# Two of eight residual additions behind two post norms, moved from VectorE to GpSimd

## The chip, the core and the metric

The kernel runs on one core of one Trainium2 chip. The metric is the device time of one execution in microseconds (us). The core has five instruction streams: TensorE (PE, matmuls; PEld, its weight loads), VectorE (DVE), ScalarE (ACT), GpSimd (POOL) and SyncE (SP, which issues the DMAs here). Each runs its own program in order, and they wait for each other on semaphores.

## The reference

Two blocks of a network are computed in a row on x of 512 tokens by 1024 features, in float32. What matters here are the residual sums of the first block, each behind a norm, and each followed by the norm and the projection of the next part:

```
x = x + rmsnorm(merged @ w_out, norm_mix_post)     # first sum
h = rmsnorm(x, norm_ffn_pre)
up = h @ w_up                                       # then a conv, a gelu gate and w_down give f
x = x + rmsnorm(f, norm_ffn_post)                   # second sum
proj = rms_norm(x, norm_a) @ w_in_a                 # start of the second block
```

rmsnorm(x) is x / sqrt(mean of x*x over the features + 1e-6), times a gain for each feature.

## The kernel before, in words

**Layout.** x lies turned in SBUF as X, [128 partitions, 8, 512]: eight "rows" m of 128 features each (the partitions), with the 512 tokens along the free dimension. "The fourth and the sixth row" are m = 3 and m = 5.

**Matmuls in three passes.** Each float32 product is made of three fp32r passes: high*high, low*high and high*low. For X that gives the pair HH (high half, made by ScalarE in `a_high`, L2086) and HL (low half, made by VectorE in `v_low`, L1273, from X and HH). Each weight block of 128 by 128 is split too: 512 KB units of eight blocks are loaded into `raw` by SyncE, ScalarE casts WH, and VectorE subtracts to get WL. TensorE needs all four.

**The norm.** The gain goes into HH and HL, and the factor 1/sqrt(...) of a token is put on after the projection, by multiplying with RS. So TensorE can start on the projection before the squares are summed. ScalarE writes the square of each row (`a_square`, L2090) into a ring SQ of two tiles (row 0 straight into SQS), GpSimd adds them up in SQS (`g_sum`, L2718), and TensorE sums SQS over the partitions (`pe_norm`).

**The stage that the change touches** is `v_post` (L1301) on VectorE with `a_post` (L2133 on) on ScalarE and `g_sum` on GpSimd. It runs twice: for "mix post" (first sum, F = FA, then the projection "ffn") and for "ffn post" (second sum, F = FB, then the projection "a"). First the factor row of the post norm is made and laid out over the partitions in PSUM (`ps("nr", st)`). Then, for each row m, VectorE computes

- TT(m) = F(m) * gain(m) * factor row, into a ring TT of two tiles (L1324),
- X(m) = X(m) + TT(m) (L1327), which it waits for its own TT(m) for,
- HL(m-1) (L1329), which needs HH(m-1) of ScalarE,

and in between, where the weight plan (`prepare`, called by `ahead` and `tile`) says so, one WL. ScalarE does HH(m) and the square of X(m), while m < 5 also a copy PW of a finished side product out of PSUM, and WH where the plan says so. GpSimd adds the square of row m to SQS. Every engine's order is fixed by the program.

**TensorE meanwhile** does eight small side tiles (`pe_post`), and then starts the next projection with a loop that takes the rows k = 0 to 7 of H one after the other, for four output tiles at once (`first` for "ffn", `tokens4` for "a"): 4 tiles x 3 passes = 12 matmuls for each k, each k waiting for HL(k) ("lo ffn" or "lo a"). The rest of the projection follows tile by tile.

**Semaphores.** Every engine has one counter (S.dve, S.act, S.pool, S.pe); `then_inc` raises it and records under the names given at which count a result is there; `wait_ge(S.dve, "x ffn", m)` waits for that count. `free(...)` names when a buffer has been read; `take` and `fill` wait for it. Each DVE, ACT and POOL instruction is made in a shared helper, so the profile's lines are those of the helpers: L151 tensor_tensor, L163 scalar_tensor_tensor, L188 copies and casts, L201 activations, L204 matmuls, L208 transposes.

Of the kernel before, what the change touches and what calls it, by code (L numbers as in the profile page):

```python
# [11 lines left out]
MUL, ADD, SUB, MAX, MIN = ALU.mult, ALU.add, ALU.subtract, ALU.max, ALU.min  # L12

P = 128
T = 512
# [542 lines left out]
def free(*name):  # L558
    return ("free", name if len(name) > 1 or isinstance(name[0], str) else name[0])


def build(nc, a_in):
    with ExitStack() as ctx:
        S = Signals(nc, ctx)
# [4 lines left out]
        def at(name, shape, dt, off=None):  # L569
            size = 4  # L570
            for d in shape[1:]:
                size *= d
            if off is None:
                off = pos[0]
                pos[0] += (size + 31) // 32 * 32
                assert pos[0] <= top, (name, pos[0], top)
            assert off + size <= top, (name, off + size, top)
            t = nc.alloc_sbuf_tensor_at(name, list(shape), dt, offset=off)
            return t[tuple(slice(None) for _ in shape)]
# [8 lines left out]
        X = at("X", [P, 8, T], F32)  # L588
        HH = at("HH", [P, 8, T], F32R)
# [77 lines left out]
        def c(name, i=0, p0=0, p1=P):  # L667
            k = COL[name] + i
            return cv[p0:p1, k:k + 1]
# [4 lines left out]
        def ring(kind, buf):  # L674
            return lambda *name: buf[:, S.place.get((kind, name), 0), :]

        tt_, sq_, th_, rt_, ct_ = ring("T", TT), ring("Q", SQ), ring("TH", TH), ring("RT", RT), ring("CT", CT)

        def col_(*name):
            k = 64 + 4 * S.place.get(("COL", name), 0)  # L680
            return sm[:, k:k + 4]
# [78 lines left out]
        def pe_columns(p, name, qs, consumed):  # L760

            s = p.fill(name[0], name[1])
            for t in range(4):
                for n, (q, sig, key) in enumerate(qs):
                    p.wait_ge(sig, *key)
                    p.matmul(s[:, t:t + 1], q[:, t * P:(t + 1) * P], ones[:, 0:1], n == 0, n == len(qs) - 1)
            p.then_inc(name[1], *consumed)

        def pe_squares(p, bank, name, sig, key, sq, consumed):

            s = p.fill(bank, name)
            p.wait_ge(S.ident, "ident")
            p.wait_ge(sig, *key)
            for t in range(4):
                p.transpose(s[:, t * P:(t + 1) * P], sq[:, t * P:(t + 1) * P], ident)
            p.then_inc(name, *consumed)

        def v_squares(v, name, col):
            v.wait_ge(S.pe, *name)
            v.tensor_reduce(col, ps(*name).rearrange("p (t s) -> p t s", s=P), ADD).then_inc(("sum",) + name, free(name))  # L780

        def pe_row(p, bank, name, col, key, consumed=()):

            s = p.fill(bank, name)
            p.wait_ge(S.ident, "ident")
            p.wait_ge(S.dve, *key)
            for t in range(4):
                p.transpose(s[:, t * P:(t + 1) * P], col[:, t:t + 1].to_broadcast([P, P]), ident)
            p.then_inc(name, *consumed)

        NORM_USE = {"a": "downed 1"}

        def pe_norm(p, st):
            def columns():
                if st in NORM_USE:
                    yield pe_squares(p, SB[4], ("nc", st), S.pool, ("sqs", st, 7), SQS, [free("sqs", st)])
                yield pe_columns(p, (SB[4], ("nc", st)), [(SQS, S.dve if st == "mix" else S.pool, ("sqs", st, 7))], [free("sqs", st)])

            p.wait_ge(S.dve, "ones")
            if st in ("p0", "p1"):  # L800
                p.mid.append(columns())
            else:
                next(columns())
            for _ in range(5 if st == "ffn" else 1):
                yield
            pe_row(p, SB[4], ("nr", st), RC, ("rc", st))
# [471 lines left out]
        def v_column(v, name, col):  # L1278
            v.wait_ge(S.act, name[0] + " sqrt", *name[1:])
            v.reciprocal(col, col).then_inc(name)  # L1280
# [20 lines left out]
        def v_post(v, st, F, post, nxt, gain):  # L1301
            v.tile(2)
            v.take("COL", ("post", st))
            v.take("COL", ("post 7", st))
            col, col7 = col_("post", st), col_("post 7", st)
            v_squares(v, ("nc", st), col)
            v_squares(v, ("nc7", st), col7)
            v.wait_ge(S.dve, "sum", "nc", st)
            v.wait_ge(S.dve, "sum", "nc7", st)
            v.tensor_tensor(col, col, col7, ADD).then_inc(("post sum", st), free("COL", ("post 7", st)))  # L1310
            v_column(v, ("post col", st), col)
            for m in range(1, 3):
                v.tile(2)
            for m in range(8):
                v.ahead(m, 4)
                v.take("T", (st, m))
                v.wait_ge(S.pe, "nr", st)
                if st == "mix post":
                    v.wait_ge(S.act, "f", m)
                    v.wait_ge(S.y[m // 2], "y")  # L1320
                else:
                    v.wait_ge(S.dve, "f2", m)
                    v.wait_ge(S.dve, "x ffn", m)
                v.scalar_tensor_tensor(tt_(st, m), F[:, m, :], c(post, m), ps("nr", st), MUL,  # L1324
                                       MUL).then_inc(("post", st, m), *([free("nr", st)] * (m == 7)))
                v.wait_ge(S.dve, "post", st, m)
                v.tensor_tensor(X[:, m, :], X[:, m, :], tt_(st, m), ADD).then_inc(("x " + nxt, m), free("T", (st, m)))  # L1327
                if m:
                    v_low(v, nxt, m - 1, gain, HH, HL)  # L1329
                if 3 <= m < EARLY:  # L1330
                    v.tile(2)
            v_low(v, nxt, 7, gain, HH, HL)
            v.soon.append(v_norm(v, nxt))
# [72 lines left out]
        def dve_program(v):  # L1406
# [292 lines left out]
            def residual(st, nk, n, x_key, nxt, gain, layer, between=None):  # L1699
                v.first(nk, n, between)  # L1700
                for m in range(8):
                    if m < n:
                        v.taken()
                    else:
                        v.tile(nk)
                    v.wait_ge(S.pe, "res", st, m)
                    v.wait_ge(S.dve, "x " + x_key, m)
                    v.tensor_tensor(X[:, m, :], X[:, m, :], ps("res", st, m), ADD).then_inc(("x " + nxt, m), free("res", st, m))
                    if m:
                        v_low(v, nxt, m - 1, gain, HH, HL)  # L1710
                v_low(v, nxt, 7, gain, HH, HL)
# [374 lines left out]
        def a_high(a, st, k, gain, hi, x_sig, *x_key):  # L2086
            a.wait_ge(x_sig, *x_key)
            a.activation(hi[:, k, :], X[:, k, :], ACT.Copy, scale=c(gain, k)).then_inc(("hi " + st, k))
# [46 lines left out]
        def a_post(a, st, nxt, gain, fin, use, layer):  # L2135
            a.tile(2)
            a.wait_ge(S.dve, "post sum", st)
            a.activation(col_("post", st), col_("post", st), ACT.Sqrt, scale=1.0 / D, bias=c("eps")).then_inc(("post col sqrt", st))
            for m in range(3):
                if m:  # L2140
                    a.tile(2)
                a_keep(a, layer, m)
            for m in range(8):
                a.ahead(m, 4)
                if m == 0:
                    a.wait_ge(S.pe, "mark", fin[0], *fin[1:])
                a_high(a, nxt, m, gain, HH, S.dve, "x " + nxt, m)
                a_square(a, nxt, m, X[:, m, :], ("sqs", st))
                if m + 3 < EARLY:
                    a.tile(2)  # L2150
                    a_keep(a, layer, m + 3)
            a.soon.append(a_norm(a, nxt, use))
# [562 lines left out]

        def g_sum(g, st, n=8):  # L2718

            for k in range(1, n):  # L2720
                g.wait_ge(S.act, "sqs in", st, k)
                if k > 1:
                    g.wait_ge(S.pool, "sqs", st, k - 1)
                g.tensor_tensor(SQS, SQS, sq_(st, k), ADD).then_inc(("sqs", st, k), free("Q", (st, k)))
# [10 lines left out]
        def pool_program(g):  # L2735
# [104 lines left out]
            g.mark("mixed")  # L2840
            g.mark("fa")
            g_sum(g, "mix post", 7)
            g_sum(g, "ffn")
            g.mark("fb")
            g_sum(g, "ffn post", 7)
            g_sum(g, "a")
            g.mark("a")
            g.wait_mark("a")
            for half in range(2):
# [377 lines left out]
```

## Time and profile before

| what | value |
| --- | --- |
| median of 3 runs | 1392.41 us (1392.0 to 1392.72) |
| the profiled execution | 1393.89 us, its span 1392.0 us |
| PE busy | 1381.5 us, 99% of the span |
| PEld busy | 1125.8 us, 81% |
| DVE busy | 841.2 us, 60% |
| ACT busy | 604.6 us, 43% |
| POOL busy | 180.3 us, 13%, 149 instructions |
| granted TensorE clock | nine tenths or more of full speed in each of 40 slices |

The profile is of one execution. The span is the time between its first and its last recorded instruction; the execution's own time is 1.89 us more. Durations of single instructions come from this execution. The releaser behind an arrow is what ended an engine's idle time. Matmuls overlap (one is recorded at 0.39 us, and the next starts 0.23 us after it), so starts say more than durations on TensorE.

### The profile page before, as it was taken

The numbers are of one execution on the slowest core, as the hardware profiler recorded it, in microseconds if no ns is written. First come the engines' busy times: TensorE is split into PE (matmuls) and PEld (weight loads), VectorE is DVE, ScalarE is ACT, GpSimd is POOL, SyncE is SP. The second block draws the span as 40 slices with busy tenths as digits, with TensorE's granted clock in tenths as the row PEclk, the third lists the DMA queues.
The fourth block names the chain that finished last, engine by engine and source line by source line (L and its number), as shares of the span: only waits on it lengthen the run. The fifth ranks groups of instructions, "written<-read, shape, count | busy, mean of one in ns | idle before, by whom it ended". The sixth has DMA issues, their size and how long they took to land.

```text
span 1392.0 us, 17342 instructions
## 1 busy us (share of the span) xinstructions
PE 1381.5 (99%) x6816; PEld 1125.8 (81%) x6816; DVE 841.2 (60%) x1223; ACT 604.6 (43%) x924; POOL 180.3 (13%) x149
## 2 busy tenths in 40 slices
PE   8999999999999999999999999999999999999998
PEld 7777777878888788888888887888888888787887
DVE  5656555755342798624676456646455565877774
ACT  5264433423235554423444345434544544344561
POOL 0300010212212300000000112000001120233330
PEclk9999999999999999999999999999999999999999
DMA  6321322222352433332333324322125233222141
GB/s 207 106 91 50 97 68 76 71 82 76 104 169 91 136 91 108 99 113 83 99 93 105 106 78 151 112 86 76 61 61 169 88 119 106 82 61 61 47 145 68
DMA packets 37554, 135.39 MB, mean 97 GB/s; under 512 B 4432, under 2 KB 5344, under 8 KB 36960
## 3 DMA queue, kind: packets, MB, share of 16 engines
q1 hardware_dynamic: 37472, 134.28, 30.5%
q8 instruction: 54, 0.88, 0.3%
q14 instruction: 28, 0.23, 0.1%
HBM read 127.97 MB, written 6.29 MB: 96 GB/s over the span
## 4 chain that ended last, share of the span: by engine, by line
PE 93%; DVE 4%; DMA 2%; issue 1%; ACT 0%; SPq 0%; DVEq 0%; ACTq 0%
PE ps L204 90%; PE ps L208 3%; DVE WL L151 1%; DVE TT L163 1%; DMA X<-in_xT 1%; DVE HL L163 1%; DMA raw<-in_wall 1%; DVE X L151 1%; SPq L211 0%; ACT WH L188 0%; DVE QT L163 0%; DVE PU L151 0%; DVE TT L157 0%; DVE sm L169 0%; DVE TT L151 0%
## 5 line engine op out<-in xcount | busy, mean ns | idle before, releaser
L204 PE MATMUL ps<-HH,WH 128*128 128x512 f32 (+1 forms) x1096 | 440.3, 402 | 2.7 <-DVE HL L163 2.0
L204 PE MATMUL ps<-HH,WL 128*128 128x512 f32 (+1 forms) x1096 | 426.1, 389 | 0.0
L204 PE MATMUL ps<-HL,WH 128*128 128x512 f32 (+1 forms) x1096 | 425.4, 388 | 0.0
L151 DVE TENSOR_TENSOR WL<-raw,WH 128x1024 fp32r<-128x1024 f32 (+1 forms) x223 | 285.8, 1286 | 85.0 <-ACT WH L188 83.9
L188 ACT CAST WH<-raw 128x1024 fp32r<-128x1024 f32 (+1 forms) x223 | 231.5, 1040 | 135.1 <-PE ps L204 112.6
L204 PEld LDWEIGHTS ps<-HH,WH 128*128 128x128 f32 x1096 | 206.1, 188 | 52.8 <-issue 8.2
L204 PEld LDWEIGHTS ps<-HH,WL 128*128 128x128 f32 x1096 | 205.8, 188 | 43.8 <-DVE WL L151 0.3
L204 PEld LDWEIGHTS ps<-HL,WH 128*128 128x128 f32 x1096 | 206.3, 188 | 41.3 <-issue 1.7
L204 PE MATMUL ps<-PH,WH 128*128 128x512 f32 x424 | 167.6, 395 | 0.0
L204 PE MATMUL ps<-PH,WL 128*128 128x512 f32 x424 | 165.2, 390 | 0.0
L204 PE MATMUL ps<-PL,WH 128*128 128x512 f32 x424 | 165.1, 389 | 0.0
L151 POOL TENSOR_TENSOR SQS<-SQS,SQ 128x512 f32<-128x512 f32 x47 | 71.8, 1528 | 681.9 <-ACT SQ L201 681.3
L151 DVE TENSOR_TENSOR TH<-ps,RS 128x512 f32<-128x512 f32 (+1 forms) x93 | 63.6, 684 | 134.8 <-PE ps L204 126.9
L204 PEld LDWEIGHTS ps<-PH,WH 128*128 128x128 f32 x424 | 79.6, 188 | 17.1 <-issue 1.0
L204 PEld LDWEIGHTS ps<-PH,WL 128*128 128x128 f32 x424 | 79.6, 188 | 16.8
L204 PE MATMUL ps<-WH,HH 128*128 128x512 f32 x224 | 92.2, 411 | 0.6 <-DVE HL L163 0.6
L204 PEld LDWEIGHTS ps<-PL,WH 128*128 128x128 f32 x424 | 79.7, 188 | 15.8
L204 PE MATMUL ps<-WL,HH 128*128 128x512 f32 x224 | 87.5, 391 | 0.0
L204 PE MATMUL ps<-WH,HL 128*128 128x512 f32 x224 | 87.3, 390 | 0.0
L201 ACT ACTIVATE TH<-TH 128x512 f32<-128x512 f32 (+1 forms) x41 | 25.5, 621 | 107.5 <-DVE TH L151 107.4
L163 DVE SCALAR_TENSOR_TENSOR CT<-TH,cv,CT 128x511 f32<-128x511 f32 x88 | 65.8, 747 | 6.4 <-ACT CT L201 4.9
L201 ACT ACTIVATE CT<-TH,cv 128x512 f32<-128x512 f32 x44 | 36.0, 817 | 56.7 <-DVE TH L151 54.9
(222 smaller groups left out, 1456.2 us busy)
## 6 DMA issues: line engine op xcount, KB each, us to landing
raw<-in_wall SPq DMA_DIRECT2D x221, 512.0 KB, 3.6
kept<-PW SPq DMA_DIRECT2D x2, 2048.0 KB, 9.1
PWR<-kept SPq DMA_DIRECT2D x2, 2048.0 KB, 8.4
X<-in_xT SPq DMA_DIRECT2D x8, 256.0 KB, 4.0
X<-in_xT SPq DMA_DIRECT2D x4, 512.0 KB, 4.7
out_T<-X SPq DMA_DIRECT2D x7, 256.0 KB, 2.0
pe<-in_pT SPq DMA_DIRECT2D x2, 512.0 KB, 4.9
DM<-in_dm SPq DMA_DIRECT2D x1, 640.0 KB, 4.2
```

Source lines behind the costliest of these rows:

```text
L151: return self.put(None if self.e is None else self.e.tensor_tensor(out, x, y, op))
L163: return self.put(self.e.scalar_tensor_tensor(out=out, in0=x, scalar=s, in1=y, op0=op0, op1=op1))
L188: return self.put(None if self.e is None else self.e.copy(out, x))
L201: return self.put(self.e.activation(out, x, f, **kw))
L204: return self.put(None if self.e is None else self.e.matmul(out, l, r, start=start, stop=stop, skip_group_check=True))
L208: return self.put(None if self.e is None else self.e.transpose(out, x, ident[0:k, 0:k]))
```

## The change

VectorE no longer adds rows 3 and 5 of X in the two stages. GpSimd does, in its own queue just ahead of the step that adds the square of that row to SQS, once VectorE's TT of the row is there. Who reads these two rows then waits for GpSimd's counter in place of VectorE's: ScalarE's HH(3) and HH(5) (L2147), the second `v_post`, which reads the X of the first (L1323), and the later residual sum of part "a" (L1707). All other rows, and the order of everything else, are as before.

```diff
+        POOL_ROWS = (3, 5)
...
@@ v_post
                     v.wait_ge(S.dve, "f2", m)
-                    v.wait_ge(S.dve, "x ffn", m)
+                    v.wait_ge(S.pool if m in POOL_ROWS else S.dve, "x ffn", m)
                 v.scalar_tensor_tensor(tt_(st, m), F[:, m, :], c(post, m), ps("nr", st), MUL,
                                        MUL).then_inc(("post", st, m), *([free("nr", st)] * (m == 7)))
-                v.wait_ge(S.dve, "post", st, m)
-                v.tensor_tensor(X[:, m, :], X[:, m, :], tt_(st, m), ADD).then_inc(("x " + nxt, m), free("T", (st, m)))
+                if m not in POOL_ROWS:
+                    v.wait_ge(S.dve, "post", st, m)
+                    v.tensor_tensor(X[:, m, :], X[:, m, :], tt_(st, m), ADD).then_inc(("x " + nxt, m), free("T", (st, m)))
@@ residual (VectorE)
-                    v.wait_ge(S.dve, "x " + x_key, m)
+                    v.wait_ge(S.pool if x_key == "a" and m in POOL_ROWS else S.dve, "x " + x_key, m)
@@ a_post
-                a_high(a, nxt, m, gain, HH, S.dve, "x " + nxt, m)
+                a_high(a, nxt, m, gain, HH, S.pool if m in POOL_ROWS else S.dve, "x " + nxt, m)
@@ g_sum
-        def g_sum(g, st, n=8):
+        def g_sum(g, st, n=8, post=None):
             for k in range(1, n):
+                if post and k in POOL_ROWS:
+                    g.wait_ge(S.dve, "post", post, k)
+                    g.tensor_tensor(X[:, k, :], X[:, k, :], tt_(post, k), ADD).then_inc(("x " + st, k), free("T", (post, k)))
                 g.wait_ge(S.act, "sqs in", st, k)
@@ pool_program
-            g_sum(g, "ffn")
+            g_sum(g, "ffn", post="mix post")
...
-            g_sum(g, "a")
+            g_sum(g, "a", post="ffn post")
```

## Rows read from the trace of the kernel before

**Rows 1.** The chain of work that ended last, its share of the span by engine.

```profile
PE 93%; DVE 4%; DMA 2%; issue 1%; ACT 0%; SPq 0%; DVEq 0%; ACTq 0%
```

**Rows 2.** Busy time: stretch, length, PE, PEld, DVE, ACT, POOL, PEclk, DMA, GB/s.

```profile
451.90:478.00 26.10, 25.52 (x111) 20.50 (x110) 25.65 (x29) 16.99 (x27) 11.81 (x7) 1.00 0.27 81
```

**Rows 3.** Timeline of TensorE, first stage: start, length in us, what, idle before.

```profile
471.88 0.39 PE L204 MATMUL ps<-HH,WL 128*128 128x512 f32 x1
472.27 0.50 PE L204 MATMUL ps<-HH,WH 128*128 128x512 f32 x1
...
474.91 0.39 PE L204 MATMUL ps<-HH,WL 128*128 128x512 f32 x1
475.87 0.47 PE L204 MATMUL ps<-HH,WH 128*128 128x512 f32 x1 [0.57 <-DVE HL L163]
```

**Rows 4.** Timeline of VectorE, first stage: WL, TT(3), X(3), HL(2), WL, X(4), and on.

```profile
457.44 2.32 DVE L151 TENSOR_TENSOR WL<-raw,WH 128x1024 fp32r<-128x1024 f32 x1
459.69 0.73 DVE L163 SCALAR_TENSOR_TENSOR TT<-FA,cv,ps 128x512 f32<-128x512 f32 x1
460.45 1.01 DVE L151 TENSOR_TENSOR X<-X,TT 128x512 f32<-128x512 f32 x1
461.39 0.74 DVE L163 SCALAR_TENSOR_TENSOR HL<-X,cv,HH 128x512 fp32r<-128x512 f32 x1
462.05 1.21 DVE L151 TENSOR_TENSOR WL<-raw,WH 128x1024 fp32r<-128x1024 f32 x1
...
463.96 1.01 DVE L151 TENSOR_TENSOR X<-X,TT 128x512 f32<-128x512 f32 x1
...
466.32 0.69 DVE L151 TENSOR_TENSOR X<-X,TT 128x512 f32<-128x512 f32 x1
466.93 1.78 DVE L163 SCALAR_TENSOR_TENSOR HL<-X,cv,HH 128x512 fp32r<-128x512 f32 x1
...
470.54 1.02 DVE L151 TENSOR_TENSOR X<-X,TT 128x512 f32<-128x512 f32 x1
471.48 0.74 DVE L163 SCALAR_TENSOR_TENSOR HL<-X,cv,HH 128x512 fp32r<-128x512 f32 x1
...
474.99 1.62 DVE L163 SCALAR_TENSOR_TENSOR HL<-X,cv,HH 128x512 fp32r<-128x512 f32 x2
```

**Rows 5.** Timeline of ScalarE, first stage: HH(4), SQ(4), PW, WH, HH(5).

```profile
465.00 0.72 ACT L201 ACTIVATE HH<-X,cv 128x512 fp32r<-128x512 f32 x1 [1.78 <-DVE X L151]
465.63 0.62 ACT L201 ACTIVATE SQ<-X 128x512 f32<-128x512 f32 x1
466.15 0.57 ACT L188 COPY PW<-ps 128x512 f32<-128x512 f32 x1
466.62 1.05 ACT L188 CAST WH<-raw 128x1024 fp32r<-128x1024 f32 x1
467.57 0.72 ACT L201 ACTIVATE HH<-X,cv 128x512 fp32r<-128x512 f32 x1
```

**Rows 6.** Timeline of GpSimd, first stage: SQS(2), SQS(3), SQS(4).

```profile
458.95 1.97 POOL L151 TENSOR_TENSOR SQS<-SQS,SQ 128x512 f32<-128x512 f32 x1 [0.27 <-ACT SQ L201]
462.82 1.60 POOL L151 TENSOR_TENSOR SQS<-SQS,SQ 128x512 f32<-128x512 f32 x1 [1.91 <-ACT SQ L201]
466.33 1.84 POOL L151 TENSOR_TENSOR SQS<-SQS,SQ 128x512 f32<-128x512 f32 x1 [1.91 <-ACT SQ L201]
```

**Rows 7.** GpSimd's other adds into X (min/median/max ns), and two timelines near 264 us.

```profile
L151 POOL TENSOR_TENSOR X<-X,TT x16: 1290/2200/2208, 264.2 to 406.2; 128x512 f32<-128x512 f32 x16
...
264.71 1.99 DVE L151 TENSOR_TENSOR gqks<-GQK,gE 128x1024 f32<-128x1024 f32 x1 [0.23 <-PE ps L204]
...
264.22 1.40 POOL L151 TENSOR_TENSOR X<-X,TT 128x512 f32<-128x512 f32 x1 [40.38 <-DVE TT L163]
265.59 2.17 POOL L151 TENSOR_TENSOR gE<-gb 128x256 f32<-128x256 f32 x2
```

**Rows 8.** Timeline of TensorE, second stage: the first matmul of row group k=6.

```profile
849.71 0.47 PE L204 MATMUL ps<-WH,HH 128*128 128x512 f32 x1 [0.58 <-DVE HL L163]
```

## The prediction, made before the changed kernel was run

> **What bounds the kernel now.** I read the chain that ended last first [rows 1]: TensorE holds 93% of it. Its matmuls follow each other every 0.227 us at the full clock of 2.4 GHz (granted 1.00 in the stage of [rows 2]), so the end of the kernel moves only where TensorE waits. The change touches two such places, the stretches behind the two sums: 451.90 to 478.00 us and 825.70 to 852.00 us. In [rows 2], the first of them, VectorE is busy for 25.65 of 26.10 us there and GpSimd for 11.81: VectorE is what the first tiles of the next projection wait for. [Rows 3] show it at TensorE, whose first loop takes the rows k of H in turn, twelve matmuls for each (four tiles of three passes). The last of k=4 starts at 471.88, so k=5 could start at 472.11; it starts at 472.27, 0.05 after HL(5) ends at 472.22 [rows 4]. Its twelve matmuls end their starts at 474.91, so k=6 could start at 475.14; it starts at 475.87, released by HL of row 6. That is 0.16 + 0.73 = 0.89 us lost. The second stage is a copy 373.84 us later: its TensorE wait is the same, at 849.71 [rows 8]. So **the most that the change can gain is 2 x 0.89 = 1.8 us**, 0.13% of the time, and what it can lose has no such limit. About 0.2% (2.8 us) is what a measurement can tell from no change.
>
> **Who waits for whom inside the stage.** For each row m VectorE does TT(m) (post norm), X(m), and HL(m-1), with WL (the low half of a weight unit) in between; ScalarE does HH(m) and the square SQ(m) after X(m); GpSimd adds SQ(m) into SQS. [Rows 4] give the lengths: TT 0.73, X 0.69, HL 0.74, WL 1.21. The next instruction starts 0.08 before the end of the last, but X starts 0.77 after TT starts, since it needs TT's result.
> The same rows hold a second fact. X(3) takes 1.01, HL(4) 1.78, one WL 2.32. Beside them stand GpSimd's adds [rows 6]: SQS(2) runs to 460.92, and X(3) ends 0.54 later, at 461.46; SQS(4) runs to 468.17, and HL(4) ends at 468.71. The other way, SQS(3), asked for at 462.82, ends 1.16 after the WL that ends at 463.26, and SQS(4) 1.16 after X(5), which ends at 467.01. TT, which reads PSUM and one tile of SBUF, stays at 0.73 beside a running add. So **an instruction of VectorE with two SBUF inputs and an add of GpSimd exclude each other**: one that waits on VectorE ends 0.55 after GpSimd's end (1.09 with 1024 columns, as WL: gqks at 264.71 ends 1.08 after the add that ends at 265.62, [rows 7]), one that waits on GpSimd 1.16 after VectorE's end. When both stand in line, the one that asked first gets it: HL(4), asked 466.93, lost to SQS(4), asked 466.33 [rows 4, 6]; and at 264.71 VectorE's gqks got in ahead of GpSimd's next add, asked 265.59 [rows 7].
>
> **The parts of the change.** *Removed:* X(3) and X(5) from VectorE, 2 x 0.69 in each stage. Without them HL(m-1) can follow TT(m) at 0.66 in place of 0.77 + 0.61, so 2 x 0.72 = 1.4 us of VectorE's queue goes. *Added:* the same two additions on GpSimd. Its add of the same tiles takes 1.29 undisturbed and 2.20 in the median [rows 7]; I take 1.29 and work the waiting out. *Moved:* X(3) stands between SQS(2) and SQS(3), X(5) between SQS(4) and SQS(5), so the squares' adds queue behind them, and HH(3) and HH(5), which ScalarE runs in order, now wait for GpSimd; with HH(5) everything behind it waits: SQ(5), a weight cast WH and HH(6). No DMA is moved. *Waits added:* VectorE waits on GpSimd's count before rows 3 and 5 of the second sum and of the later residual; those X are hundreds of us old, so between 0 and 0.03 us each (the gap from the end of X(4), 464.97, to the start of the HH(4) that it releases, 465.00 [rows 4, 5]), and I take 0. TT(5) and TT(7) now need GpSimd to have read TT(3) and TT(5): by the working below they are read at 462.6 and 471.3 and rewritten at 466.5 and 475.0, so nothing waits.
>
> **The replay of the first stage**, with these durations, from TT(3) on, which still starts at 459.69 [rows 4].
> HL(2) is asked for at 460.36, waits for SQS(2) (end 460.92), ends 461.47. GpSimd's X(3), next in its queue, was asked before WL (461.39) and ends at 461.47 + 1.16 = 462.63. WL ends 1.09 later, 463.72 (before: 463.26). HH(3) can start at 462.66, 1.2 us after the old X(3)'s end; with the steps of [rows 5] (HH to SQ 0.63, SQ to the next 0.52, then PW 0.47, WH 0.95) SQ(3) ends at 463.95 and SQS(3) runs from 464.03 to 465.32. TT(4) starts 463.64; X(4), asked at 464.41, ends at 465.87 (before: 464.97). So **one row in, the stage is 0.9 us late, not early**: 0.45 + 1.2 + 0.8 of waiting against 0.7 saved.
> HL(3) 465.79 to 466.53. TT(5) starts 466.46; no X(5); HL(4) is asked at 467.13, its HH(4) being done at 466.63, and ends at 467.87. SQS(4), asked at 467.24, ends at 469.03. WL, asked at 467.80, ends at 470.12. X(5), asked at 469.0, ends at 471.28. TT(6) starts 470.04, X(6) is asked at 470.81 and ends at 471.83 (before: 471.56). HH(5) runs from 471.32 to 472.04, so HL(5) ends at 472.83 (before: 472.22). SQS(5), asked at 472.65, ends at 473.99; WL, asked at 472.76, ends at 475.08; TT(7) starts 475.00; SQS(6), asked near 474.7, ends at 476.24; X(7), asked at 475.77, at 476.79. HL(6) starts at 476.71, **1.72 us later than the 474.99** of [rows 4]. TensorE follows: k=5 starts 0.6 late, k=6 1.7 late, and HL(7), due at 480.3, is ready at 478.4.
> The contest of HL(4) and SQS(4) is close (0.1 us). Had SQS(4) won, the same rules put HL(5)'s end at 474.1 and HL(6)'s start at 476.9, 1.9 late. Both outcomes give 1.7 to 1.9.
> Behind HL(6) nothing absorbs it. The last WL ends 1.7 later, as does the norm's last square sum, and the norm row goes through TensorE, which is late by as much. TensorE's waits of [rows 3] and [rows 8] are for HL; I find none for a freed bank or for weights in either stage. SyncE's weight loads and the store of PW behind them wait for WL, and WL is late by no more than TensorE. So the delay goes to the end in full.
> **Sum:** 2 x 1.72 = 3.4 us, between 3.4 and 3.8. It stands against the profiled execution (span 1392.0, 1393.89 with what lies around it, 1.5 above the median of the three runs, 1392.41). Put on the median: **1395.8 us**, +0.25%.
> Beside these rows a rule of the Trainium skill (page GPSIMD Engine Reference, section Engine selection) advises VectorE for elementwise work, since GpSimd is about 2 times slower with two inputs; the trace has 1.29 against 0.69, which agrees. Charged as length alone it would give 4 x 0.60 = 2.4 us, less than the replay, which also counts the mutual waiting.
>
> **Rivals.**
> *A. The contests fall more kindly: +1.6.* The place is 461.4, where WL and GpSimd's X(3) both stand behind HL(2). If GpSimd's request really comes after WL's (it then starts its add later than its record), WL ends at 462.6, X(3) at 463.8, X(4) at 464.3, and the rest by the same rules: HL(5) in time for TensorE, HL(6) starting at 475.8. TensorE's k=6 is then 0.8 late: 1394.0. For it: starts on GpSimd are rough. Against: GpSimd's next add starts within 0.1 us of the last one's end (264.22 + 1.40, 265.59, [rows 7]), 0.4 us ahead of WL.
> *B. Not slower: VectorE gains its two slots and loses nothing for them.* The price is at most the 1.8 us of the waits in [rows 3]: 1390.6. The mechanism is that GpSimd's longer queue overlaps TT and ScalarE's waits and never stands ahead of VectorE; the point that decides is the start of HL(6): before 474.99 it gains, from 474.26 on down it gains all. For it: VectorE is full (25.65 of 26.10 us) while GpSimd is idle for over half [rows 2]. Against: the seven SQS adds already stretch a WL to 2.32 and HL(4) to 1.78, and HH(5) would still have to wait for GpSimd.
> The Trainium skill (Perfetto Trace Analysis, Optimizing Scalar/DVE Operations) says that moving work to GpSimd may make sense when VectorE is saturated, but that between these two it might not help, because of a shared port. By its first half this rival wins, by its second the forecast; the stretched rows speak for the second.
> *C. More than the replay: +5 to +8.* The k=6 wait grows from 0.7 to about 2.4 us. If the granted clock fell after it, matmuls at 1.2 GHz would follow at twice 0.227 us, so that every ten of them cost 2.3 us. Or a third wait appears behind the norm. For it: no wait of this length stands in these stages before. Against: the clock stays at 1.00 through the two waits of today [rows 2, 3].
> *D. The change does nothing visible* would need both sums' HL chains to have slack; [rows 3] show that they have none.
>
> **How the numbers follow.** Forecast 0.56, A 0.24 (with its neighbours, +0.5 to +2.6), B 0.08, C 0.12. Slower by over 0.2% (above 1395.2): most of the forecast's case and C, 0.60. Within 0.2%: A, the low end of the forecast and B, whose whole gain is under 2.8 us, 0.37. Faster: 0.03. The range leaves out B's best and most of C: 1392.2 to 1397.6. The forecast's own range is 1395.2 to 1396.6.
>
> **What would show it.** In the changed profile: two POOL X<-X,TT in each stage, recorded at 1.7 to 2.3 us; VectorE X down from eight to six per stage, the WL behind TT(3) stretched to about 2.3, the one behind HL(4) as well; ScalarE idle some 2.7 us before HH(5), released by POOL; HL(6) starting 1.7 later against the stage's start; TensorE's wait before k=6 at 1.9 to 2.4 us in place of 0.57, and one of about 0.6 before k=5. If HL(6) starts by 475.0, the exclusion or its order is wrong; if it is 1.7 late and the end is not 3.4 later, something downstream absorbs it.

## The result, and the profile after

The changed kernel takes 1395.71 us (median of 9 runs, 1395.39 to 1397.11) against 1392.72 us (9 runs, 1392.0 to 1394.92) for the kernel before: a ratio of 1.002 with a 95% interval of 1.0012 to 1.0028, or 1.7 to 3.9 us slower. 1395.8 us was forecast. The profiled execution took 1395.99 us, with a span of 1394.2 us.

In the table "k=5" and "k=6" are the starts of the first matmul that reads row 5 or row 6. The stages are measured from the start of their own TT(0), since the first stage begins at another time in every execution (450.6 to 452.9 us over the profiles of this study, more on that at the end).

| | before | after |
| --- | --- | --- |
| TT(0) of the first stage starts | 451.94 | 450.95 |
| TensorE's k=5 behind TT(0) | 20.33 | 20.83 |
| HL(6) behind TT(0) | 23.05 | 24.63 |
| TensorE's k=6 behind TT(0), first / second stage | 23.93 / 23.95 | 25.52 / 25.53 |
| from the first stage's TT(0) to the second's | 373.82 | 375.41 |
| from the second stage's TT(0) to the end of the span | 566.24 | 567.84 |

Each stage costs 1.59 or 1.60 us more, and all of it arrives at the next stage and at the end: 3.2 us. The span grew by only 2.2 because this execution reached the first stage 0.99 us earlier.

The timeline of TensorE in the first stage (start, length, what, idle before and its releaser), which answers to [rows 3]:

```profile
470.91 0.39 PE L204 MATMUL ps<-HH,WL 128*128 128x512 f32 x1
471.78 0.50 PE L204 MATMUL ps<-HH,WH 128*128 128x512 f32 x1 [0.48 <-DVE HL L163]
...
476.47 0.47 PE L204 MATMUL ps<-HH,WH 128*128 128x512 f32 x1 [1.67 <-DVE HL L163]
```

Two waits stand where there was one that the profile marked: 0.48 before k=5 and 1.67 before k=6, in place of 0.57. The second stage has the same (this answers to [rows 8]):

```profile
851.89 0.47 PE L204 MATMUL ps<-WH,HH 128*128 128x512 f32 x1 [1.66 <-DVE HL L163]
```

The busy time in the same stretch of the span as [rows 2]:

```profile
451.90:478.00 26.10, 23.95 (x105) 19.15 (x104) 25.56 (x26) 16.75 (x26) 14.11 (x9) 1.00 0.25 81
```

VectorE has fewer instructions in the stretch (26 against 29) and is as busy as before (25.56 us against 25.65). The stage lies 0.99 us earlier in this execution; a stretch of the same length that starts with its own TT(0), at 450.95, gives 25.52 and 26 as well. What was taken from VectorE came back as waiting inside its instructions, as its timeline shows, from TT(3) on; it answers to [rows 4]:

```profile
458.69 0.73 DVE L163 SCALAR_TENSOR_TENSOR TT<-FA,cv,ps 128x512 f32<-128x512 f32 x1
459.35 1.12 DVE L163 SCALAR_TENSOR_TENSOR HL<-X,cv,HH 128x512 fp32r<-128x512 f32 x1
460.39 2.31 DVE L151 TENSOR_TENSOR WL<-raw,WH 128x1024 fp32r<-128x1024 f32 x1
462.62 0.73 DVE L163 SCALAR_TENSOR_TENSOR TT<-FA,cv,ps 128x512 f32<-128x512 f32 x1
463.39 1.42 DVE L151 TENSOR_TENSOR X<-X,TT 128x512 f32<-128x512 f32 x1
...
466.05 0.74 DVE L163 SCALAR_TENSOR_TENSOR HL<-X,cv,HH 128x512 fp32r<-128x512 f32 x1
466.72 2.32 DVE L151 TENSOR_TENSOR WL<-raw,WH 128x1024 fp32r<-128x1024 f32 x1
...
469.73 1.00 DVE L151 TENSOR_TENSOR X<-X,TT 128x512 f32<-128x512 f32 x1
470.98 0.75 DVE L163 SCALAR_TENSOR_TENSOR HL<-X,cv,HH 128x512 fp32r<-128x512 f32 x1 [0.24 <-ACT HH L201]
471.64 2.32 DVE L151 TENSOR_TENSOR WL<-raw,WH 128x1024 fp32r<-128x1024 f32 x1
...
475.58 1.62 DVE L163 SCALAR_TENSOR_TENSOR HL<-X,cv,HH 128x512 fp32r<-128x512 f32 x2
```

And GpSimd's, which answers to [rows 6]: SQS(2), X(3), SQS(3), SQS(4), X(5), SQS(5).

```profile
457.96 1.96 POOL L151 TENSOR_TENSOR SQS<-SQS,SQ 128x512 f32<-128x512 f32 x1 [0.28 <-ACT SQ L201]
459.88 1.74 POOL L151 TENSOR_TENSOR X<-X,TT 128x512 f32<-128x512 f32 x1
462.97 1.29 POOL L151 TENSOR_TENSOR SQS<-SQS,SQ 128x512 f32<-128x512 f32 x1 [1.36 <-ACT SQ L201]
466.17 1.78 POOL L151 TENSOR_TENSOR SQS<-SQS,SQ 128x512 f32<-128x512 f32 x1 [1.91 <-ACT SQ L201]
467.92 2.27 POOL L151 TENSOR_TENSOR X<-X,TT 128x512 f32<-128x512 f32 x1
471.54 1.34 POOL L151 TENSOR_TENSOR SQS<-SQS,SQ 128x512 f32<-128x512 f32 x1 [1.35 <-ACT SQ L201]
```

Read the two side by side. HL(2), asked for at 459.35, ends at 460.47, 0.55 after SQS(2) ends at 459.92. X(3) on GpSimd ends at 461.62, 1.15 after HL(2). WL, asked for at 460.39, has to wait for it and ends at 462.70, 1.08 later. The moved addition has made one weight unit take 2.31 in place of 1.21. The same happens to the WL behind HL(4) (466.72, behind SQS(4)) and to the one behind HL(5) (471.64, behind SQS(5)), while HL(4) no longer waits (0.74 against 1.78 in [rows 4]).

The whole delay can be added up from the two timelines of VectorE between TT(0) and HL(6). Against the lengths without a contest (X 0.69, HL 0.74, WL 1.21) its instructions take 3.4 us longer in the kernel before and 6.2 us longer after, and after there is some 0.3 us of idleness in front of HL(5), where HH(5) is late. So 3.0 us of waiting were added, and HL(6) starts 1.58 later (24.63 against 23.05): what the two moved additions gave back is the difference, 1.4 us.

ScalarE meanwhile waits for GpSimd before HH(5), as the second of these rows shows:

```profile
466.46 1.05 ACT L188 CAST WH<-raw 128x1024 fp32r<-128x1024 f32 x1
470.22 0.73 ACT L201 ACTIVATE HH<-X,cv 128x512 fp32r<-128x512 f32 x1 [2.70 <-POOL X L151]
```

### The profile page after: what moved, and what is told of

Its sections match the earlier page's. It is cut to its first block, busy times and chain, and to the rows that moved or that the text cites. A ratio compares the mean times of both kernels' runs of the same rounds, so it can differ in the third digit from the quotient of the medians.

```text
span 1394.2 us, 17344 instructions
## 1 busy us (share of the span) xinstructions
PE 1381.6 (99%) x6816; PEld 1125.8 (81%) x6816; DVE 844.8 (61%) x1219; ACT 604.6 (43%) x924; POOL 186.3 (13%) x153
## 4 chain that ended last, share of the span: by engine, by line
PE 94%; DVE 3%; issue 1%; DMA 1%; POOL 1%; ACT 0%; SPq 0%; DVEq 0%; ACTq 0%
PE ps L204 91%; PE ps L208 3%; DVE WL L151 1%; DVE TT L163 1%; DVE X L151 1%; DVE HL L163 0%; DMA raw<-in_wall 0%; POOL X L151 0%; POOL SQS L151 0%; DMA X<-in_xT 0%; ACT HH L201 0%; DVE QT L163 0%; ACT SQ L201 0%; DVE TH L151 0%; ACT WH L188 0%
## 5 line engine op out<-in xcount | busy, mean ns | idle before, releaser
L151 DVE TENSOR_TENSOR WL<-raw,WH 128x1024 fp32r<-128x1024 f32 (+1 forms) x223 | 293.8, 1322 | 84.2 <-ACT WH L188 82.9
```

Source lines behind the costliest of these rows:

```text
L151: return self.put(None if self.e is None else self.e.tensor_tensor(out, x, y, op))
```

## The experiments

Two theories, and a third beside them. **P**: VectorE's instructions with two SBUF inputs and GpSimd's adds exclude each other, first come first served, and the sum of these contests decides. A "replay" is this rule worked through, instruction by instruction, from rows of a trace. **L**: GpSimd's add is simply longer, and nothing excludes anything. **S**: what costs is that HH(5) comes late. Kernels with repeated runs are given with the ratio to the kernel before, run on the same chip, and its 95% interval; an interval that takes in 1 shows no difference by itself, and there the distances inside the profile carry the argument. dummy_set and thin_after have one run each and are read by their profiles alone.

### One row alone: row3_only and row5_only

```diff
-        POOL_ROWS = (3, 5)
+        POOL_ROWS = (3,)      # row3_only; (5,) in row5_only
```

> Only row 3 is moved to GpSimd, in both stages. Measure: from the start of TT(0) to the start of TensorE's k=6, which is 23.93 and 23.95 us before and 25.52 and 25.53 after. Theory P (VectorE's instructions with two SBUF inputs and GpSimd's adds exclude each other, first come first served): the same replay gives 24.8 in each stage, +0.87, so 1.7 us for the kernel; WL behind TT(3) at 2.3, HL(2) at 1.1. Rival L (GpSimd's add is merely 0.60 us longer and on the path, nothing excludes anything): +0.6 per stage, 1.2 us, WL unstretched. Rival S (only the late HH(5) costs): nothing, or a gain of up to 0.9 per stage.

> Only row 5 is moved, in both stages. Theory P: X(5) on GpSimd ends about 470.4 on the old time axis, HL(5) is in time, and k=6 starts at 24.76 behind TT(0), +0.8 per stage, 1.6 us for the kernel. Rival L: +0.6 per stage, 1.2 us. Rival S (only the late HH(5), and the weight cast and HH(6) behind it, cost): the whole +1.6 per stage, 3.2 us.

Measured: row 3 alone 1.0011 (1.0001 to 1.0021), k=6 at 24.77 and 24.76 behind TT(0), +0.83 a stage. Row 5 alone 1.0009 (0.9999 to 1.0018), k=6 at 24.68 and 24.68, +0.74. The replay had 24.8 and 24.76. The waits of TensorE in the first stage, row3_only:

```profile
471.78 0.50 PE L204 MATMUL ps<-HH,WH 128*128 128x512 f32 x1 [0.42 <-DVE HL L163]
475.37 0.47 PE L204 MATMUL ps<-HH,WH 128*128 128x512 f32 x1 [0.58 <-DVE HL L163]
```

and row5_only, where k=5 is in time and only k=6 waits:

```profile
475.99 0.47 PE L204 MATMUL ps<-HH,WH 128*128 128x512 f32 x1 [1.63 <-DVE HL L163]
```

S is out: row 5, which moves the addition that HH(5) waits for, costs no more than row 3, which does not. L's 0.6 a stage is nearer, but its unstretched WL is refuted: in row3_only the WL behind TT(3), at 460.06, takes 2.31. The two halves add up, 0.83 + 0.74 = 1.57 against 1.59.

### The adds without the move: dummy_add and dummy_set

```diff
@@ g_sum of the kernel before; VectorE keeps all its additions
+                if post and k in (3, 5):
+                    g.wait_ge(S.dve, "post", post, k)
+                    g.tensor_tensor(DUM[post], tt_(post, k), tt_(post, k), ADD).then_inc(("dum", post, k), free("T", (post, k)))
@@ in dummy_set the last line is
+                    g.memset(DUM[post], 0.0).then_inc(("dum", post, k), free("T", (post, k)))
```

> VectorE keeps all eight X additions; GpSimd does two further adds per stage at the places of the moved ones, TT + TT of rows 3 and 5 into a tile that nobody reads. So nobody waits for their result, and no work leaves VectorE. Theory P: the adds cost VectorE their port time at unlucky places: k=6 starts about 26.9 behind TT(0), +3.0 per stage, about 6 us for the kernel, twice what the change cost. Rivals L and S (length or lateness of the result): nobody needs the result, so 0.0, 23.95.

> As dummy_add, but the two further GpSimd instructions per stage fill the tile with zero, and read nothing. It tells a queue that is merely longer from one that reads SBUF. If only an instruction that reads SBUF excludes VectorE's: k=6 stays at 23.9 to 24.0 behind TT(0) in both stages and no VectorE instruction is stretched beside the fills. If any GpSimd instruction excludes VectorE: up to the length of the fill more (not known, an estimate is 0.3 to 1.3 us each).

Measured: dummy_add 1.0022 (1.0013 to 1.0032), k=6 at 25.56 and 25.55, +1.6 a stage, and 375.45 between the stages. Nobody reads the result and no work is moved, and yet it costs 1.6 us a stage; by L and S it should cost nothing. That this is just what the change cost is chance: P gave twice as much, and two smaller effects, told below, took it down. The ring of TT adds no wait here: GpSimd is through with TT(3) and TT(5) at 462.85 and 470.88, and VectorE writes over them from 466.81 and 475.39. In dummy_set (one run, 1394.13 us) nothing moved: k=6 at 23.92 and 23.93, 373.82 between the stages, as before.

GpSimd's timeline in dummy_add, first stage:

```profile
461.36 1.49 POOL L151 TENSOR_TENSOR rst<-TT 128x512 f32<-128x512 f32 x1
463.30 2.38 POOL L151 TENSOR_TENSOR SQS<-SQS,SQ 128x512 f32<-128x512 f32 x1 [0.46 <-ACT SQ L201]
...
469.39 1.49 POOL L151 TENSOR_TENSOR rst<-TT 128x512 f32<-128x512 f32 x1
```

and VectorE's beside it, HL(2) and the WL behind it:

```profile
461.87 1.52 DVE L163 SCALAR_TENSOR_TENSOR HL<-X,cv,HH 128x512 fp32r<-128x512 f32 x1
463.31 1.21 DVE L151 TENSOR_TENSOR WL<-raw,WH 128x1024 fp32r<-128x1024 f32 x1
```

GpSimd's and then VectorE's in dummy_set, at the same place:

```profile
461.35 0.52 POOL L191 MEMSET rst<- 128x512 f32 x1
...
461.88 0.74 DVE L163 SCALAR_TENSOR_TENSOR HL<-X,cv,HH 128x512 fp32r<-128x512 f32 x1
462.54 1.21 DVE L151 TENSOR_TENSOR WL<-raw,WH 128x1024 fp32r<-128x1024 f32 x1
```

With the add HL(2) takes 1.52, with the fill 0.74. The fill (461.35 to 461.87) lies inside VectorE's X(3) (460.94 to 461.95), which takes 1.01 as in the kernel before, where SQS(2) alone held it up. So a further instruction in GpSimd's queue costs nothing here when it only fills a tile; one that reads SBUF does. That agrees with the Trainium skill (SBUF — State Buffer, Who interferes with whom): a VectorE instruction with two SBUF inputs contends with a GpSimd instruction that reads SBUF, not with one that only writes it.

The size was missed, +3.0 expected and +1.6 measured, for two reasons. The dummy adds end 0.91 after VectorE's end (HL(4) ends at 469.97, the add at 470.88), not 1.16: adding one tile to itself is a quarter of a us shorter. And one contest was a tie. SQS(3) is recorded from 463.30, the WL from 463.31, and WL went first (1.21, unstretched, while SQS(3) took 2.38). By record the replay gives it to GpSimd: WL would end at 465.64 in place of 464.52, and X(4), after it, at 467.02 in place of 466.23, so about 0.8 us more a stage (an estimate from these rows). Together with the two shorter adds, about 0.5 us, that is nearly all of the 1.4 that was missed. The second stage has the same tie (838.75 and 838.76) with the same outcome. In other runs an X and an SQS are recorded within 0.01 us of each other, and VectorE went first each time. That GpSimd's record starts somewhat before its request would explain it, but no run tests that; contests within some hundredths of a us could not be forecast from the starts here.

### Taking the contests away: thin_after and wl_late_after

```diff
@@ thin_after, g_sum of the changed kernel
+                w = 8 if post else T
-                g.tensor_tensor(SQS, SQS, sq_(st, k), ADD)
+                g.tensor_tensor(SQS[:, 0:w], SQS[:, 0:w], sq_(st, k)[:, 0:w], ADD)
@@ wl_late_after, v_post of the changed kernel; wl_late has it in the kernel before
             for m in range(8):
+                if m == 5:
+                    v.lead = AHEAD - 2
...
             v_low(v, nxt, 7, gain, HH, HL)
+            v.lead = AHEAD
```

> The changed kernel, with the seven additions of squares on GpSimd in each of the two stages cut from 512 to 8 columns, so the two following norms are not the reference's. GpSimd is left with the two moved X and seven short adds. Theory P: without the long square adds the moved X cost VectorE less than they save: k=6 starts at 22.9 behind TT(0), on time, in both stages, -1.05 per stage against before and -2.6 against the change. Rival L (the moved adds' own length, with HH(3) and HH(5) late, is the cost): 24 or more.

> The changed kernel (rows 3 and 5 on GpSimd) with the same two WL moved behind HL(7). Two of the contests that the change lost (WL behind SQS(4), WL behind SQS(5)) are then gone. Theory P, replayed: k=6 starts 23.1 behind TT(0), k=5 20.4, so -0.8 per stage against before and +0.2 against wl_late; the kernel -1.7 us against before. Rival L (length alone, 1.2 per stage): 24.1.

> Kernel before, with VectorE's two WL behind HL(4) and HL(5) moved behind HL(7); they are for weights that TensorE needs 6 us later. Theory P: what TensorE waits for is VectorE's queue ahead of HL(5) and HL(6), so both waits vanish: k=5 at 20.17, k=6 at 22.89 behind TT(0), -1.0 to -1.1 per stage, -2.1 us for the kernel. If a late WL or the later load and store behind it costs TensorE a wait further on, the gain is smaller, and that wait shows between the stages.

thin_after leaves out nearly all of the norms' sums of squares, so it is a probe and not a version to use (one run, 1390.1 us). It has no wait in either stage, TensorE busy for the whole of it, as the stretch shows:

```profile
451.00:477.00 26.00, 26.00 (x116) 21.50 (x116) 21.74 (x27) 16.98 (x26) 6.55 (x9) 1.00 0.32 106
```

372.65 us lie between the stages and 565.01 behind the second, 2.8 us under the change in each, where P had 2.6, and 1.17 and 1.23 under the kernel before. With the square adds out of the way the two moved additions make TensorE wait for nothing, though the WL behind HL(2) still takes 2.31 beside one of them: VectorE is busy 21.74 of 26 us. So what the moved adds cost, they cost in a stage that the square adds have already filled. The kernel before with thin square adds was not run, so thin_after doesn't say what the move alone gains.

wl_late and wl_late_after did inside the stages what was expected: in wl_late TensorE waits for no HL in either stage, in wl_late_after k=5 starts at 20.30 and k=6 at 23.19, without a marked wait. **As a whole both missed**, and what wl_late's last sentence left room for came, larger than the gain: wl_late 1.0023 (1.0014 to 1.0032), wl_late_after 1.004 (1.0026 to 1.0054). The gain was eaten behind the stages, by waits of TensorE for a WL: 2.99 and 0.83 us in wl_late, 3.73 and 1.72 in wl_late_after. TensorE in wl_late, 49 us behind the first TT(0):

```profile
496.45 0.39 PE L204 MATMUL ps<-HH,WL 128*128 128x512 f32 x1
499.83 0.77 PE L204 MATMUL ps<-HH,WH 128*128 128x512 f32 x1 [2.99 <-DVE WL L151]
500.39 0.63 PE L204 MATMUL ps<-HL,WH 128*128 128x512 f32 x1
500.82 0.63 PE L204 MATMUL ps<-HH,WL 128*128 128x512 f32 x1
501.25 0.63 PE L204 MATMUL ps<-HH,WH 128*128 128x512 f32 x1
```

A wait of 2.99 us for a WL, and behind it matmuls that follow at 0.43 in place of 0.227. The profile's stretches, with the granted clock third from the end:

```profile
480.00:499.00 19.00, 16.84 (x76) 13.54 (x75) 8.22 (x13) 7.41 (x11) 0.00 (x0) 1.00 0.39 151
499.00:503.00 4.00, 3.17 (x8) 2.59 (x9) 3.93 (x7) 1.84 (x3) 0.00 (x0) 0.57 0.48 131
```

TensorE's clock had fallen to its lower level, 1.2 GHz (0.57 is the mean of the stretch), and came back within 3 us. The wait and the slow matmuls together cost about 4.5 us (an estimate from the starts: 3.38 us between two matmuls, then 2.70 for six, in place of 0.227 for each), against 1.17 gained inside the stage (k=7 at 25.60 behind TT(0) against 26.77); the stages lie 377.29 us apart, 3.5 more than before. The chain to that WL goes through two engines that the replay leaves out: SyncE may load a raw unit only when the WL three units before is done, and behind these loads, in the same queue, it stores PW; ScalarE's first activation into CT waits for that store to land, and the next weight casts stand behind it in ScalarE's queue. In the kernel before and in wl_late the activation started behind these waits:

```profile
488.20 0.82 ACT L201 ACTIVATE CT<-TH,cv 128x512 f32<-128x512 f32 x1 [1.87 <-DMA kept<-PW]
489.52 0.82 ACT L201 ACTIVATE CT<-TH,cv 128x512 f32<-128x512 f32 x1 [5.69 <-DMA kept<-PW]
```

The first line is 36.3 us behind its TT(0), the second 38.9. Of these 2.6 us only 0.7 are a later issue of the store (28.1 against 27.4 behind TT(0)); the rest is a longer transfer, 10.7 us from issue to landing against 8.8. The late loads just ahead of it in the queue are the likely cause of that, which no run separates.

### A move at the right row: row7_only

```diff
-        POOL_ROWS = (3, 5)
+        POOL_ROWS = (7,)
```

> Row 7 alone is moved to GpSimd, in both stages: HL(6), which TensorE waits for, no longer has X(7) in front of it, and only HL(7), due 2.7 us later, waits for the moved addition. Theory P, replayed: k=6 starts 23.2 behind TT(0) (before 23.93), k=7 about 25.95, 0.2 late; -0.75 per stage, -1.5 us for the kernel. Rival L (a move costs its longer add wherever it stands): +0.6 per stage, 1.2 us slower.

Measured: 0.9996 (0.9988 to 1.0005), no difference that shows, where 1.5 us less was expected. In the stages it came nearly as replayed: k=6 starts 23.26 and 23.27 behind TT(0) (23.2 expected) without a marked wait, k=7 at 26.10 (25.95 expected). Behind the second stage the gain holds (565.43 us to the end against 566.24). Behind the first it was lost: 374.53 between the stages, +0.7, with a new wait on the same chain.

```profile
498.56 0.47 PE L204 MATMUL ps<-HH,WH 128*128 128x512 f32 x1 [1.10 <-DVE WL L151]
```

### Moving the store: three kernels and a fourth

```diff
@@ sp_program; row7_store_early (with row 7 on GpSimd), store_early (kernel before), late_store_early (wl_late)
+            keep(0)
             s.first(8, 4)
-            keep(0)
@@ row7_store_mid (with row 7 on GpSimd)
-            s.first(8, 4)
+            s.first(6, 4)
             keep(0)
+            s.first(2, 4)
```

> Row 7 alone on GpSimd, and SyncE's 2 MB store of PW (first layer) issued ahead of the weight loads of the next projection's start, in place of behind them. In row7_only TensorE gained its wait before k=6 and gave 1.10 us back 25 us later, waiting for a WL that stands behind ScalarE's wait for this store. If the store is that cause: no wait there, the second stage starts 372.9 us after the first (before 373.82), and the kernel is 1.9 us faster than before (ratio 0.9986). If the cause is another, the wait of 1.1 us stays.

> Kernel before, with only the store moved. Control: TensorE's waits in the stage are for HL and stay, k=6 at 23.9 behind TT(0); 373.8 between the stages; no change in time, 0.0 us within 0.3. If the store in front of the loads makes a weight late, a new wait for WL appears behind the first stage.

> wl_late with the store moved as well. In wl_late two waits for WL (3.0 and 0.8 us), behind each stage one, and a fall of the clock behind the longer one, ate the gain. If the first of them is the store's place: it vanishes, the stages lie 372.8 us apart, and the kernel is about 3.5 us faster than wl_late; the wait behind the second stage stays, so it ends about 1 us below before at best. If the late loads themselves are the cause, the 3.0 us wait stays.

All three missed; only store_early's last sentence allowed for a weight made late. Measured: 1.0023 (1.0014 to 1.0032), 1.0018 (1.0008 to 1.0027) and 1.0021 (1.001 to 1.0032), with 377.2 us between the stages in each. The long wait for WL behind the first stage is gone and a larger wait is inside the stage. TensorE in row7_store_early:

```profile
478.89 0.77 PE L204 MATMUL ps<-HH,WH 128*128 128x512 f32 x1 [2.61 <-DVE HL L163]
```

and what SyncE (start, length) and ScalarE did there:

```profile
467.73 0.33 SPq L211 DMA_DIRECT2D kept<-PW  x1
...
476.29 1.04 ACT L188 CAST WH<-raw 128x1024 fp32r<-128x1024 f32 x1 [6.50 <-PE ps L204]
477.24 0.72 ACT L201 ACTIVATE HH<-X,cv 128x512 fp32r<-128x512 f32 x1
```

SyncE held back four loads until PW's last tile was there, and sent them behind 2 MB. The cast WH in front of HH(6) then starts at 476.29. The profile names TensorE for its wait, but TensorE was through with that buffer some 6 us earlier, since in row7_only the same cast starts 17.7 us behind TT(0) and here 23.4. What came last was the load, which late_store_early names at the same place:

```profile
475.63 1.04 ACT L188 CAST WH<-raw 128x1024 fp32r<-128x1024 f32 x1 [6.47 <-DMA raw<-in_wall]
```

How much of it is the holding back and how much the 2 MB in front, no run separates. HH(6), HL(6) and TensorE follow, and here too matmuls go at 0.43 behind the wait.

> Row 7 alone on GpSimd, and the store of PW one weight load earlier (before it came behind five loads of the stage, in row7_store_early ahead of four; now only the last load comes after it). If the store's place in SyncE's queue is what cost row7_only its 1.10 us wait: the store is issued near 21.7 behind TT(0) in place of 28.5, ScalarE no longer waits for it, TensorE waits nowhere between the stages, these lie 372.9 us apart (before 373.82), and the kernel is 1.9 us faster than before (ratio 0.9986). If the store collides with a weight load that is needed, a wait for HL or WL of 1 to 3 us appears, as in row7_store_early, and the kernel is slower.

Measured: 1391.49 us (11 runs) against 1393.75 us for the kernel before on the same chip, **0.9985 (0.9976 to 0.9994), faster than the kernel before**. The changed kernel was not run beside it; by the spans it lies 4.2 us above (1394.2 against 1390.0). The store goes out 21.9 us behind TT(0), and the activation follows its input, not the store:

```profile
473.14 0.42 SPq L211 DMA_DIRECT2D kept<-PW  x1
...
485.83 0.81 ACT L201 ACTIVATE CT<-TH,cv 128x512 f32<-128x512 f32 x1 [0.83 <-DVE TH L151]
```

The two largest of the seven entries for TensorE's waits over the whole span; no entry is for a WL:

```profile
PE ps L204 <- POOL rst L191: 1.5, 1, 1.5
PE ps L204 <- DVE HL L163: 1.0, 2, 0.8
```

The profile accounts for 1.3 us of it: 373.16 between the stages (-0.66) and 565.57 behind the second (-0.67). The two medians lie 2.3 us apart; the profile of one execution doesn't account for the rest. 372.9 was expected between the stages. The lateness of k=5 is unchanged (20.33, where thin_after has 20.16), its twelve matmuls take 2.94 us in place of 2.72, and HL(6), at 1.13 beside SQS(6), lets k=6 start at 23.27, where thin_after has it at 22.88. Further gain was there: thin_after got 1.17 and 1.23.

## Why the prediction was right

**The forecast** was 1395.8 us by a delay of 1.72 us in each stage; the runs gave 1395.71 and the profile 1.59. That the two totals agree to 0.1 us is partly luck: the two delays measured in the profiles sum to 3.2 us, just under the 3.4 to 3.8 of the forecast, the medians lie 2.99 apart, and the kernel before came out at 1392.72 in place of the 1392.41 that the 3.4 was put on. Against TT(0) the steps came as follows, forecast and measured: X(3) ends 10.69, 10.67; the WL behind it 11.78, 11.75; X(4) 13.93, 13.86; HL(4) is asked for at 15.19, 15.10; X(5) ends 19.34, 19.24; HL(5) 20.89, 20.78; X(7) 24.85, 24.71; HL(6) starts 24.77, 24.63. The order of every contest in this chain was right, the close one of HL(4) (466.05) and SQS(4) (466.17) too. The 0.14 us of difference gathered in small steps, a few hundredths each.

**"Exclude each other"** is confirmed by dummy_add against dummy_set, with the addition that GpSimd's instruction must read SBUF. **"The one that asked first gets it"** held in the two stages of every run wherever the two starts lie 0.1 us or more apart; where they lie within 0.01 us VectorE went first, in dummy_add against the order on record. **"1.4 us of VectorE's queue goes"** came true: it is what the change gave back against 3.0 us of new waiting, as added up above.

**"Behind HL(6) nothing absorbs it"** was right: 1.59 us arrive at the second stage and 1.60 at the end. The sentence on SyncE's store was right for the change and hid how thin that cover is: a stage that ends 0.7 us earlier already loses to it, as row7_only shows.

**The rivals.** A, the kinder contest behind HL(2), did not happen: X(3) (459.88) went ahead of WL (460.39). B, no loss from GpSimd, is out by the stretched rows. C, a fall of the clock, did not happen behind the wait of 1.67 us, granted 1.00 throughout the stretch. Where it did happen, in wl_late and the three early stores, a matmul cost 0.43 us as C had it, but for six matmuls only, some 1.3 us in all (2.70 for six starts against 1.36).

**Two sums of the prediction were off**, without changing the forecast. The bound on the gain, 1.8 us, is too low: thin_after gained 1.17 and 1.23 us in the same stages, 2.4 together. The 0.89 counted the two gaps and left out that the twelve matmuls behind them take 2.87 and 2.84 us in place of 2.72 (20.33 to 23.20 and 23.93 to 26.77 behind TT(0)), which adds 0.27 in each stage. And the wait before k=6 was put at 1.9 to 2.4 us, where 1.67 was measured: with k=5 itself late by 0.6, the prediction's own starts give 0.57 + 1.72 - 0.6, about 1.7.

## What to carry to other kernels

Before work is moved from VectorE to GpSimd, list VectorE's instructions with two SBUF inputs beside GpSimd's, and replay both queues. In this kernel an add on GpSimd that waited ended 1.15 us after VectorE's instruction, and a VectorE instruction that waited ended 0.55 us (512 columns) or 1.09 us (1024) after GpSimd's. What is moved should be the piece behind which the critical result no longer has to stand; X(7) was that, X(3) and X(5) were not. And after a stage is made earlier, look for the next cover along the other queues: here a store in the load queue. With row 7 moved, issuing it one load earlier made the way between the stages 1.4 us shorter (373.16 against 374.53), and issuing it four loads earlier made it 2.7 us longer (377.24).

## What the runs showed of the hardware that was not expected

- GpSimd's fill of 128x512 took 0.52 us and ran beside VectorE's X(3), which took 1.01 as without it; an add of a tile to itself is 0.25 us shorter than one of two tiles (0.91 against 1.16 behind VectorE's end).
- Waits of TensorE of 3.73, 2.99, 2.90 and 2.61 us were each followed by about six matmuls at 0.43 us, waits of 1.67 and 1.29 us by matmuls at full rate, 0.23 to 0.24 us apart from the second on.
- The first stage begins at 450.6 to 452.9 us from one execution to the next, for much the same work ahead of it. A wait of TensorE for HL between 20 and 100 us, where x and the first weights are still being loaded, makes most of it: 0.8 us in the profile before, none in the one after, 1.6 in dummy_add, 1.5 in dummy_set. With an effect of 3 us, a span compared with a span would have been a third off; distances between two places of one profile agree to 0.02 us.
